# Mixing stage of a hybrid decoder layer: the order of the query blocks reversed

## The reference

```
# memory branch, chunk by chunk, carry (C, n, m)
s = einsum('bhtd,bhsd->bhts', qb, kb) * dmat
num = einsum('bhts,bhsv->bhtv', s, vb) + w_inter * einsum('bhvd,bhtd->bhtv', C, qb)
C_new = w_prev * C + einsum('bhs,bhsv,bhsd->bhvd', w_s, vb, kb)
# attention branch, a block of 128 queries at a time; blocks are independent
visible = key_pos[None, :] <= qpos[:, None]
_, sel = top_k(indexer_scores(iqb, iwb, ik, visible), topk)
s = where(valid, q . k_sel * B_HD ** -0.5, -inf);  o = softmax(s) . v_sel
```

## Time and profile before

| | |
|---|---|
| median of 3 runs | 4029.04 us |
| profiled execution | 4025.62 us, span 4024.0 us |
| TensorE busy | 3868.4 us (96%), granted clock 0.983 in the mean |
| VectorE, ScalarE, GpSimd busy | 2919.6 (73%), 1416.1 (35%), 1674.3 us (42%) |
| DMA | 368.40 MB, 92 GB/s in the mean |
| mixing stage, last projection matmul to last matmul | 2207.6 to 3052 us |
| first transpose of blocks 0, 1, 2, 3, 4 | 2233.5, 2260.2, 2290.7, 2320.2, 2352.7 us |
| first transpose of block 15 | 2986.0 us |

### The profile page before, as it was taken

One profiled execution on the slowest core, in us unless ns is written; L12 is line 12 of the kernel. 1 busy time (PEld: TensorE's weight loads), 2 busy tenths in 40 slices (PEclk: granted clock), 3 DMA queues, 4 the chain that ended last, 5 costly groups with the idle time before them and its releaser, 6 DMA issues. The chain is left out here.

```text
span 4024.0 us, 41948 instructions
## 1 busy us (share of the span) xinstructions
PE 3868.4 (96%) x14560; PEld 2310.2 (57%) x14560; DVE 2919.6 (73%) x3888; ACT 1416.1 (35%) x2619; POOL 1674.3 (42%) x1531
## 2 busy tenths in 40 slices
PE   6899999999999999999999799999998899999999
PEld 3555555564456566666666566555553788854444
DVE  4589999779999999999997566555454577653333
ACT  4411211156234323433331566555553322111111
POOL 0000036449687556666664332122103666552111
PEclk8999999999999999999999899999999999999999
DMA  5312223330111121121111733222232855531111
GB/s 220 91 55 69 67 71 90 112 135 36 60 60 64 54 71 64 63 70 63 64 62 63 194 115 103 66 90 78 61 101 80 228 167 168 173 128 68 39 52 46
DMA packets 289713, 368.40 MB, mean 92 GB/s; under 512 B 72515, under 2 KB 217179, under 8 KB 286302
## 3 DMA queue, kind: packets, MB, share of 16 engines
q1 hardware_dynamic: 249106, 249.79, 20.3%
q0 software_dynamic: 19664, 86.31, 5.8%
q10 hardware_dynamic: 20736, 29.66, 2.3%
HBM read 235.11 MB, written 129.28 MB: 91 GB/s over the span
## 5 line engine op out<-in xcount | busy, mean ns | idle before, releaser
L1315 DVE MAX8 best<-score 128x8 f32<-128x384 f32 (+13 forms) x448 | 639.7, 1428 | 23.4 <-POOL score L1283 8.5
L1317 DVE MATCH_REPLACE8 score<-best,score 128x384 f32<-128x384 f32 (+13 forms) x448 | 631.1, 1409 | 0.0
L1072 PE MATMUL pr<-xnT,w_row 128*128 128x347 f32 (+1 forms) x960 | 298.7, 458 | 0.0
L396 PE MATMUL pg<-xnT,wt 128*128 128x416 f32 x800 | 282.4, 516 | 0.0
L1224 POOL TENSOR_TENSOR kT<-kT 128x347 f32<-128x347 f32 (+1 forms) x240 | 194.1, 809 | 211.6 <-ACT kT L1142 204.6
L1703 PE MATMUL mix_slot<-mix_kT,mix_bq 128*128 128x512 f32 (+3 forms) x640 | 271.5, 540 | 7.6 <-DVE mix_sd L2042 3.4
L1742 PE MATMUL mix_po<-mix_probT,mix_v 128*128 128x512 f32 x544 | 240.2, 595 | 5.2 <-ACT mix_probT L1842 4.3
L1072 PEld LDWEIGHTS pr<-xnT,w_row 128*128 128x128 f32 x960 | 180.6, 190 | 106.7 <-issue 11.7
L1142 ACT COPY kT<-pr 128x347 f32<-128x347 f32 (+1 forms) x240 | 106.7, 446 | 352.1 <-PE pr L1072 341.9
L396 PEld LDWEIGHTS pg<-xnT,wt 128*128 128x128 f32 x800 | 152.9, 191 | 127.9 <-issue 127.9
L1224 POOL TENSOR_TENSOR kT<-kT,sm 128x347 f32<-128x347 f32 (+1 forms) x179 | 160.1, 895 | 125.0 <-ACT sm L1142 122.1
(11 more groups left out here) (648 smaller groups left out, 8063.2 us busy)
## 6 DMA issues: line engine op xcount, KB each, us to landing
gt_scr<-kT SPq DMA_DIRECT2D x40, 694.0 KB, 3.3
out_gm<-gt_scr ACTq DMA_DIRECT2D x32, 520.0 KB, 4.8
gt_scr<-kT SPq DMA_DIRECT2D x20, 692.0 KB, 4.2
wt<-in_w_in SPq DMA_DIRECT2D x22, 512.0 KB, 4.1
w0a<-in_w_in SPq DMA_DIRECT2D x11, 1024.0 KB, 6.6
w_row<-in_w_in SPq DMA_DIRECT2D x10, 1024.0 KB
qt_scr<-kT POOLq DMA_DIRECT2D x8, 1040.0 KB, 4.3
early<-ybt_scr SPq DMA_DIRECT2D x4, 2080.0 KB, 9.8
```

Source lines behind the costliest of these rows:

```text
L396: ins = nc.tensor.matmul(pg[0:m, g, 0:GW], w[:, k, 0:m], c["xnT"][:, k, g * GW:(g + 1) * GW], start=k == 0, stop=k == KT - 1)
L1072: ins = nc.tensor.matmul(pr[:, b, 0:w], lhs, rhs, start=k == 0, stop=k == 3)
L1315: nc.vector.max(best[:, :], sc).then_inc(top_step, 1)
L1317: nc.vector.match_replace(sc, best[:, :], sc, TAKEN).then_inc(top_step, 1)
```

## The change

The query blocks are walked from 15 down to 0. Three orders (`BLOCK_ORDER`, `GROUP_ORDER`, `HEAD_ORDER`) and their inverses replace the formulas in i and hd wherever semaphores, buffers and parities are counted. The memory branch keeps its order: memory step n+1 now stands in the n-th block of the new order, so step 1 in block 15 and step 15 in block 1. Sample events keep their step numbers. The keys are loaded in two halves of 8 tiles ahead of memory step 1, the values in two halves behind it, and block 14's queries and mask last. The last value store is that of block 0.

```diff
-FIRST_KEYS = 4
+FIRST_KEYS = 8
+BLOCK_ORDER = [NB - 1 - n for n in range(NB)]
+GROUP_ORDER = [(b, kv) for b in BLOCK_ORDER for kv in range(KV)]
+HEAD_ORDER = [(b, BH // KV * kv + x) for b, kv in GROUP_ORDER for x in range(BH // KV)]
+BLOCK_AT = {b: n for n, b in enumerate(BLOCK_ORDER)}
+GROUP_AT = {g: n for n, g in enumerate(GROUP_ORDER)}
+HEAD_AT = {h: n for n, h in enumerate(HEAD_ORDER)}
...
-    heads = [(i, hd) for i in range(NB) for hd in range(BH)]
+    heads = HEAD_ORDER
...
-        if i + 1 < NB:
-            m, *x = memory[hd]
-            events.append((m, i + 1, *x))
-        elif hd in (1, 2):
-            events.append(("L", hd - 1))
+        step, at = n // BH + 1, n % BH
+        if step < NB:
+            m, *x = memory[at]
+            events.append((m, step, *x))
+        elif at in (1, 2):
+            events.append(("L", at - 1))
...
-            def load_a(i):
-                p, rows = i % 2, slice(i * P, (i + 1) * P)
-                if i >= 2:
-                    after_slot(sp, ("S", i - 2, BH - 1, key_pieces(i - 2) - 1))
+            def load_a(n):
+                i, p = BLOCK_ORDER[n], n % 2
+                rows = slice(i * P, (i + 1) * P)
+                if n >= 2:
+                    earlier = BLOCK_ORDER[n - 2]
+                    after_slot(sp, ("S", earlier, BH - 1, key_pieces(earlier) - 1))
...
-            load_resident(0, FIRST_KEYS)
+            load_keys(0, FIRST_KEYS)
+            load_keys(FIRST_KEYS, NB)
             load_m(1)
+            load_values(0, FIRST_KEYS)
+            load_values(FIRST_KEYS, NB)
             load_a(1)
-            load_resident(FIRST_KEYS, NB)
...
-                    pe.wait_ge(a_loaded[p], 32 * (i // 2 + 1))
-                    pe.wait_ge(k_resident[i >= FIRST_KEYS], 16)
+                    pe.wait_ge(a_loaded[p], 32 * (n // 2 + 1))
+                if hd == 0:
+                    pe.wait_ge(k_resident[q], 16)
...
-                    pe.wait_ge(v_resident[i >= FIRST_KEYS], 16)
+                    for x in range(2):
+                        pe.wait_ge(v_resident[x], 16)
...
-                    if i:
-                        act.wait_ge(inverse, BH * (i - 1) + hd + 1)
+                    if n >= BH:
+                        act.wait_ge(inverse, n - BH + 1)
```

More of the change, by code:

```diff
@@ L1412, in mixing_events @@
             events.append(("E", *heads[n + AHEAD - 1]))
-        if hd == 5 and i + 1 < NB:
-            events.append(("Q", i + 1))
+        if at == 5 and step < NB:
+            events.append(("Q", step))
         if hd % 4 == 3:
@@ L1542, in store_oT @@
         def store_oT(eng, i, kv):
-            n = 2 * i + kv
+            n = GROUP_AT[i, kv]
             eng.dma_start(d["ybt"][4 * kv:4 * kv + 4, :, i * P:(i + 1) * P].rearrange("t p q -> p t q"),
@@ L1615, in _ @@
             sp.wait_ge(oT_ready, 2 * NB)
-            store_oT(sp, NB - 1, 1)
+            store_oT(sp, *GROUP_ORDER[-1])
         @block.gpsimd
@@ L1669, in _ @@
                     pool.dma_start(d["y"][rows, 0:D].rearrange("q (h e) -> q h e", h=AH), ya[:, :, :]).then_inc(ya_stored, 16)
-                elif e[0] == "O" and 2 * i + e[2] + 1 < 2 * NB:
-                    pool.wait_ge(oT_ready, 2 * i + e[2] + 1)
+                elif e[0] == "O" and GROUP_AT[i, e[2]] + 1 < len(GROUP_ORDER):
+                    pool.wait_ge(oT_ready, GROUP_AT[i, e[2]] + 1)
                     store_oT(pool, i, e[2])
@@ L1738, in _ @@
                             pe.wait_ge(bank_free[x], (last + 2 - x) // 2)
-                    if 2 * i + kv:
-                        pe.wait_ge(oT_ready, 2 * i + kv)
+                    if GROUP_AT[i, kv]:
+                        pe.wait_ge(oT_ready, GROUP_AT[i, kv])
                     for t in range(i + 1):
@@ L1838, in copy_group @@
             act.wait_ge(turned, n + 1)
-            if hd % 4 == 0 and 2 * i + hd // 4:
-                act.wait_ge(o_mm, 2 * i + hd // 4)
+            if hd % 4 == 0 and GROUP_AT[i, hd // 4]:
+                act.wait_ge(o_mm, GROUP_AT[i, hd // 4])
             t0, t1 = 4 * q, min(4 * q + 4, i + 1)
@@ L1862, in _ @@
                 if kind == "E":
-                    hd = e[2]
-                    act.wait_ge(nbias_ready, BH * i + hd + 1)
-                    if i:
-                        act.wait_ge(inverse, BH * (i - 1) + hd + 1)
-                    nc.scalar.activation(prob[(BH * i + hd) % AHEAD][:, 0:(i + 1) * P], prob[(BH * i + hd) % AHEAD][:, 0:(i + 1) * P], ACT.Exp,
-                                         scale=SCALE, bias=mx[:, (BH * i + hd) % AHEAD, 1:2], accum_out=sums[:, hd:hd + 1]).then_inc(p_ready, 1)
+                    n = HEAD_AT[i, e[2]]
+                    act.wait_ge(nbias_ready, n + 1)
+                    if n >= BH:
+                        act.wait_ge(inverse, n - BH + 1)
+                    scores = prob[n % AHEAD][:, 0:(i + 1) * P]
+                    nc.scalar.activation(scores, scores, ACT.Exp, scale=SCALE, bias=mx[:, n % AHEAD, 1:2],
+                                         accum_out=sums[:, n % BH:n % BH + 1]).then_inc(p_ready, 1)
                 elif kind == "T":
@@ L1872, in _ @@
                     kv = e[2]
-                    act.wait_ge(o_mm, 2 * i + kv + 1)
-                    n = 2 * i + kv
+                    n = GROUP_AT[i, kv]
+                    act.wait_ge(o_mm, n + 1)
                     if n >= 2:
@@ L1959, in _ @@
                 if kind == "S":
-                    hd = e[2]
-                    q, b = e[3], (BH * i + hd) % AHEAD
+                    n, q, at = HEAD_AT[i, e[2]], e[3], BLOCK_AT[i]
+                    b = n % AHEAD
                     lo, width = pieces((i + 1) * P)[q]
@@ L1964, in _ @@
                     if q:
-                        after_slot(dve, ("S", i, hd, q - 1))
+                        after_slot(dve, (*e[:3], q - 1))
                     else:
-                        dve.wait_ge(a_loaded[p], 32 * (i // 2 + 1))
-                    if BH * i + hd >= AHEAD:
-                        j, hp = divmod(BH * i + hd - AHEAD, BH)
+                        dve.wait_ge(a_loaded[at % 2], 32 * (at // 2 + 1))
+                    if n >= AHEAD:
+                        j, hp = HEAD_ORDER[n - AHEAD]
                         dve.wait_ge(turned, bank_no[("T", j, hp, min(2 * q + 1, key_groups(j) - 1))] + 1)
                     nc.vector.tensor_tensor_reduce(out=prob[b][:, lo:lo + width], in0=slot[:, s, 0:width],
-                                                   in1=mk[p][:, lo:lo + width], scale=1.0,
+                                                   in1=mk[at % 2][:, lo:lo + width], scale=1.0,
                                                    scalar=mx[:, b, 0:1] if q else TAKEN, op0=ALU.add, op1=ALU.max,
```

23 lines of the change are left out of this document (13 added, 10 removed).

## The result

The changed kernel takes **4040.28 us** (median of 9 runs, 4035.97 to 4044.97) beside 4027.88 for the kernel before on the same chip (9 runs): a ratio of 1.0034, 95% interval 1.0023 to 1.0044. It is slower, and its time lies just above the range. The profiled executions are 10.8 us apart (4036.41 and 4025.62 us, so 3.9 and 2.3 under the two medians; spans 4034.8 and 4024.0), and 10.3 of these lie in the mixing stage, from the end of the last projection matmul to the first matmul of the next phase: 857.1 us against 846.8.

What follows compares the result with a forecast made beforehand. Stage bound by TensorE in large blocks, by chains through other engines and DMA in the first 80 us; lost time 54.9 to 50.9 us, a gain of 4 from 4029.0, gave 4025 us, range 4014 to 4040.

Steps and rivals of the forecast that it cites:

- Blocks 2 to 14 keep a memory step each, and I leave their lost time as it is.: Middle blocks: lost time (time less TensorE work at full clock) unchanged, apart from 0.8 us more in block 2.
- Its own sign of being wrong: Listed as showing the forecast wrong: the middle blocks' (4 to 14) lost time not 37 us.
- block 2's gathers: Block 2: sample value rows bring two gathers a step on GpSimd, nearly binding; +0.8 us, ends 0 and 4.
- Start: Stage start to first transpose: keys arrive later behind other loads; transpose near 2248, 40.3 us with 23.4 lost.
- Block 15: Block 15, now first and with memory step 1: loses 3 us, like blocks 4 to 14.
- Block 1: Block 1 with memory step 15: 23.5 us, 8 lost, ends 3 and 12; the ScalarE and TensorE chain stays.
- The rival of the falling clock: Last small blocks: TensorE's clock falls, half clock for half of block 1, +8 us, 4033; chance 0.10.
- The wait for the decay product: Block 1: the earlier 4.31 us wait, put down to a decay row late in the crowded start, goes.
- Hand-over: Block 0's first transpose to next phase: 20.5 us, 15.7 lost; the next phase's first matmul waits for eight state loads.
- the rest of the weight load: Hand-over: what is left of the 4 MB weight load ahead of the state loads adds 1.5 us.
- The rival of 4038: Hand-over binds: weight load whole before state loads if issues under 13 us apart, SP's queue holds barrier; +13 us; 0.13.
- Sum: Lost time of start, blocks 15, 1, 0 with hand-over, plus block 2's 0.8: 54.9 before, 50.9 after, gain 4 us.

Runs made afterwards that it cites:

- rev_swap: Changed kernel with the 4 MB weight load issued on SP's queue behind the eight state loads instead of ahead of them: 4048.41 us, ratio 1.0053.
- rev_dup: Changed kernel with the first group of transposes of each head in blocks 2 to 6 made twice: 4047.01 us, one execution.
- old_dup: Kernel before with the first group of transposes of each head in blocks 2 to 6 made twice: 4040.37 us, one execution.
- old_light: Kernel before with turning and score product of sample key rows 1 to 31 made for one key group of two: 4017.71 us, ratio 0.9978.
- rev_light: Changed kernel with turning and score product of sample key rows 1 to 31 made for one key group of two: 4028.71 us, 1.0006 of the kernel before.
- rev_s4: Changed kernel with all sample events and the next phase's weight load 8 head steps earlier: 4040.54 us, one execution.

## Why the prediction was wrong

**The step that failed** is one clause: "Blocks 2 to 14 keep a memory step each, and I leave their lost time as it is." It cost 12.3 us (44.6 lost before, 56.9 after, by the table's blocks; +16.5 in blocks 2 to 6, -1.0 in block 7, -3.2 in blocks 8 to 14). Its own sign of being wrong came: blocks 4 to 14 lost 44 us and not 37. The reasoning took lost time for a property of a block, when it is what is left of a chain once TensorE's own work has covered part of it. The first part had counted 22 key rows in the middle blocks and never asked in which blocks they would lie afterwards: that a step number keeps its sample event was taken for nothing moving, while for a block of a given size everything at its head steps is exchanged, and the scores of the block behind it too. The one step in this direction, block 2's gathers (+0.8, ends 0 and 4), had the right place and engine; +3.0 came, in one execution (rev_swap has 1.2 more).

How the chain shows in the changed kernel: ScalarE at the end of block 3, from the last of four squares on, and TensorE's value product behind it.

```profile
2981.78 1.28 ACT L1953 ACT_TABLE_LOAD   x1
2983.08 0.30 ACT L1953 ACTIVATE mix_den<-mix_den,eps 128x4 f32<-128x4 f32 x1
2983.28 0.56 ACT L1861 COPY mix_probT<-mix_pg 128x512 f32<-128x512 f32 x1
2983.87 1.28 ACT L1887 ACT_TABLE_LOAD   x1
...
2985.77 0.56 ACT L1861 COPY mix_probT<-mix_pg 128x512 f32<-128x512 f32 x1
```
```profile
2986.59 3.67 PE L1761 MATMUL mix_po<-mix_probT,mix_v 128*128 128x512 f32 x8 [1.68 <-ACT mix_probT L1861]
```

TensorE has ended all it has before by 2984.91 and then waits 1.68 us for a copy that stands behind two table loads. The row in that head step is a value row of 0.36 now; a key row there had 0.44 or 0.87. What the runs show is that work in blocks 2 to 6 is partly covered in both orders (rev_dup, old_dup, old_light), so that their time did not follow the 17.4 us that left them. By the worth of a microsecond in blocks 3 to 6 (0.46) some 9 of the 16.5 us lost there are explained, as an estimate; the rest is open, the late place included. How much each part has of the 12.3 is not settled either. Half of the key-row work accounts for 3 us of the orders' difference in blocks 2 to 14 (they shortened by 6.9 in old_light and 9.9 in rev_light). The root accounts for none on balance: without it these blocks shortened by 11.5 in the old order and 11.0 in the reversed, for block 2 took back what blocks 3 to 6 had given. Waits for value gathers are 2.1 us in blocks 5 to 2.

**The other steps.**
- *Start:* predicted first transpose 2248, 23.4 lost and 4 to 5 us idle before the first scores; 2246.86, 21.0 and 4.88. The mechanism stands as told, a wait for the keys in the queue (the earlier trace rows has 1.94 there) and then eight passes that ran mostly at half clock (5.88 us, where four take 1.72 at full clock):
```profile
2226.04 5.88 PE L1721 MATMUL mix_slot<-mix_kT,mix_bq 128*128 128x512 f32 x8 [4.88 <-DMA mix_kT<-qt_scr]
```
- *Block 15:* predicted 3 lost, measured 5.0. Mis-sized by 2.
- *Block 1:* predicted 23.5 us and clock near 1; 27.6 at clock 0.86. In rev_dup the same block had clock 1.00 and took 24.7, so some 3 us are the clock and 1.2 the term itself. The rival of the falling clock was right in this block, and in blocks 2 and 3 not in the profiled execution (both at 1.00) but in others: 0.94 and 0.95 in rev_swap, 3 us together. It is the likely reason, though not shown, that the median lies 3.9 us above the profiled execution (of the nine runs the one of 4035.97 us has a mean clock of 0.983, the one of 4044.97 has 0.979). The wait for the decay product was not the crowded start's alone, as I had it: 2.06 us of it stand in block 1 again.
- *Hand-over:* predicted 20.5 us, measured 19.4. The prediction had the matmul released by the state's landing. That landing came 0.26 us ahead of the matmul, so the mechanism stands, but as half of a tie that the prediction did not see: the stores on SP's queue behind the eight loads, and the barrier behind them, end at the same time. The 1.5 us for the rest of the weight load were 0.9 (15.70 against 14.8 us on the queue). The rival of 4038 named that queue, and its deciding point was passed (9.9 us between the issues, under 13), but its price did not come. The swap shows that what stands on the queue behind the loads can cost more than the loads.
- *Sum:* start and blocks 15, 1 and 0 went from 54.8 to 52.6 us lost, where the prediction had 54.9 to 50.1 and 0.8 for block 2. So they gained 2.2; the 12.3 above turned that into a loss of 10.1. (A small slip: 633.3 less 597 is 36.3 and not 36.8; it changes nothing.)

So the sign was lost in the part that had no working at all. A row at hand could have warned: in block 2 of the old order TensorE was busy 26.28 of 29.5 us, with ScalarE and VectorE each at 20 in a chain with waits between them, so what would happen when work left TensorE there was an open question and wanted two ends, not a zero.

## What to carry to other kernels

When an order changes, list for every block what will stand beside it, not only what is in it: filler work in a stretch that another engine's chain nearly binds is worth a part of its price (0.46 here at full clock), and the same filler elsewhere costs more (0.60). Two table loads that stood together between the transposes and their copies cost more than the same two with a copy between them, and most of it in the large blocks, in part through the clock. Look at the clock of each small block in more than one execution before arguing from 2 or 3 us. Before loads are moved to the end of a phase, count how long they need to be issued and to land, and what their queue must issue behind them before the barrier.

## What the runs showed of the hardware

- Eight loads of 0.5 MB were 13.09 us on SP's queue in the kernel before, 14.76 and 14.79 in rev_s4 and rev_swap, 15.70 behind the weight load, each time with the DMA engines at a share of 0.95 or more; a store behind the 4 MB weight load stood on it for 8.04.
- The granted clock fell behind waits. Block 3's value product (eight passes) took 3.67 us behind a wait of 1.68 in the changed kernel and 5.37 behind one of 1.84 in rev_swap; six passes took 5.46 behind a wait of 2.94 in rev_s4 and 2.81 behind one of 0.94 in the changed kernel.
- Four products of 32 stationary columns took 0.36 us for eight passes, two passes alone 0.33. The Trainium skill (TensorE: Matmul & The Clock Gate, Part 3: Packing small matmuls) says that tiles of the array run concurrently, and the trace agrees; I had read it only afterwards, and counted eight passes as work that could be halved.
- exp and ln each brought a table load of 1.28 us. The Trainium skill (ScalarE: Activation LUTs, Table sets: the hidden batching unit) names one set with both, so that ln and then exp would need one load; here it was not so, and the measurement decides.
